# An unused buffer of 320 bytes ahead of the activation tiles: their addresses move by 192 within 512

## What is computed

```python
def swiglu_ffn(x, w_in, w_out):
    gate, up = jnp.split(x @ w_in, 2, axis=-1)       # w_in 1024 x 5632
    return (jax.nn.silu(gate) * up) @ w_out          # w_out 2816 x 1024

def first_block(x, ...):
    for i in range(2):
        if i == 1:
            kv = shared_kv(h, ...)
        h = h + 0.5 * swiglu_ffn(rmsnorm(h, ffn1_norm[i]), ffn1_w_in[i], ffn1_w_out[i])
        hn = rmsnorm(h, mix_norm[i])
        h = h + (short_conv_mixer(hn, ...) if i == 0 else nsa_mixer(hn, ..., kv))
        h = h + 0.5 * swiglu_ffn(rmsnorm(h, ffn2_norm[i]), ffn2_w_in[i], ffn2_w_out[i])
    return h

def second_block(x, ...):
    for layer in range(2):
        h = rms_norm(x, pre_norm[layer])
        m = even_mixer(h, ...) if layer == 0 else odd_mixer(h, ...)
        x = x + rms_norm(m, post_norm[layer])
    return x
```

## The kernel before

| buffers | offset before | after |
|---|---|---|
| raw_a, raw_b, wah, wal, wbh, wbl, hres, cst | 128 | 128 |
| arena, t384 | 160 | 160 |
| rt, rstd, tmp, gate_hid | 320 | 320 |
| hidh, hidl, hnh, hnl, zero, rms | 320 | 128 |
| pbuf, ptb, nmx | 352 | 160 |

## Time and profile before

### The profile page before, as it was taken

One profiled execution on the slowest core, in us unless ns is written; L12 is line 12 of the kernel. 1 busy time (PEld: TensorE's weight loads), 2 busy tenths in 40 slices (PEclk: granted clock), 3 DMA queues, 4 the chain that ended last, 5 costly groups with the idle time before them and its releaser, 6 DMA issues.

```text
span 1378.7 us, 27592 instructions
## 1 busy us (share of the span) xinstructions
PE 1307.9 (95%) x10717; PEld 1248.1 (91%) x10717; DVE 843.6 (61%) x1365; ACT 610.4 (44%) x871; POOL 503.9 (37%) x533
## 2 busy tenths in 40 slices
PE   7999999989999998999999889999999997889878
PEld 6999999989999998999999668999999996788758
DVE  5675458786445566444446784744446586775575
ACT  5343344344334344333335575533334436434381
POOL 3455533315554433444440252444441002600052
PEclk8999999999999999999998899999999999989999
DMA  8787655658676555666644115666653554334300
GB/s 255 210 240 214 202 167 159 185 160 238 204 226 200 168 161 172 204 186 185 183 128 152 36 36 153 184 183 183 183 183 108 153 154 160 111 95 149 124 31 32
DMA packets 275115, 222.52 MB, mean 161 GB/s; under 512 B 8098, under 2 KB 256438, under 8 KB 274924
## 3 DMA queue, kind: packets, MB, share of 16 engines
q1 hardware_dynamic: 272528, 215.59, 51.5%
q0 software_dynamic: 1504, 4.49, 1.6%
q10 hardware_dynamic: 1020, 1.58, 0.4%
HBM read 216.40 MB, written 4.19 MB: 160 GB/s over the span
## 4 chain that ended last, share of the span: by engine, by line
PE 80%; DVE 9%; ACT 5%; POOL 2%; issue 2%; DMA 1%; ACTq 0%; DVEq 0%; SPq 0%; POOLq 0%
PE psum L712 24%; PE psum L713 24%; PE psum L714 24%; DVE wal L1664 2%; DVE hnl L1682 1%; POOL wal L2293 1%; ACT hnh L1294 1%; ACT wah L1213 1%; DVE wal L1847 1%; POOL wbl L2293 1%; ACT pbuf L1461 1%; DVE rstd L1646 1%; PE psum L960 1%; PE psum L914 1%; DVE arena L1725 1%
## 5 line engine op out<-in xcount | busy, mean ns | idle before, releaser
L712 PE MATMUL psum<-hnh,wah 128*128 128x256 f32 (+1 forms) x2176 | 620.3, 285 | 12.2 <-DVE wal L1664 6.6
L713 PE MATMUL psum<-hnl,wah 128*128 128x256 f32 (+1 forms) x2176 | 612.2, 281 | 0.0
L714 PE MATMUL psum<-hnh,wal 128*128 128x256 f32 (+1 forms) x2176 | 611.7, 281 | 0.0
L2293 POOL TENSOR_TENSOR wbl<-raw_b,wbh 128x256 fp32r<-128x256 f32 x412 | 401.6, 1004 | 480.6 <-ACT wbh L1220 409.8
L712 PEld LDWEIGHTS psum<-hnh,wah 128*128 128x128 f32 (+1 forms) x2176 | 416.0, 191 | 18.7 <-issue 12.1
L713 PEld LDWEIGHTS psum<-hnl,wah 128*128 128x128 f32 (+1 forms) x2176 | 414.3, 190 | 2.3 <-issue 1.7
L714 PEld LDWEIGHTS psum<-hnh,wal 128*128 128x128 f32 (+1 forms) x2176 | 415.8, 191 | 0.0
L1664 DVE TENSOR_TENSOR wal<-raw_a,wah 128x2048 fp32r<-128x2048 f32 (+1 forms) x128 | 290.9, 2272 | 101.2 <-ACT wah L1213 99.9
L1213 ACT ACTIVATE wah<-raw_a 128x2048 fp32r<-128x2048 f32 (+1 forms) x126 | 237.2, 1884 | 96.5 <-PE psum L714 81.6
L1332 ACT ACTIVATE gate_hid<-tmp 128x256 f32<-128x256 f32 x88 | 36.7, 417 | 434.7 <-DVE tmp L1782 434.7
L712 PE MATMUL psum<-hidh,wbh 128*128 128x256 f32 x768 | 214.4, 279 | 1.2 <-DVE hidl L1718 1.2
(11 more groups left out here) (304 smaller groups left out, 1468.8 us busy)
## 6 DMA issues: line engine op xcount, KB each, us to landing
raw_a<-in_ffn_w_in SPq DMA_DIRECT2D x176, 512.0 KB, 5.0
raw_b<-in_ffn_w_out SPq DMA_DIRECT2D x88, 512.0 KB, 4.4
raw_a<-in_w_in_even SPq DMA_DIRECT2D x15, 1024.0 KB, 5.3
raw_a<-in_conv_w_in SPq DMA_DIRECT2D x24, 512.0 KB, 3.9
raw_a<-in_w_in_odd SPq DMA_DIRECT2D x11, 1024.0 KB, 5.3
raw_a<-in_w_kv SPq DMA_DIRECT2D x6, 1024.0 KB, 5.5
raw_b<-in_conv_w_out SPq DMA_DIRECT2D x8, 512.0 KB, 5.6
raw_a<-in_attn_w_q SPq DMA_DIRECT2D x4, 1024.0 KB, 5.3
```

Source lines behind the costliest of these rows:

```text
L712: mm(dst, wh, xh, start=start, stop=False)
L713: mm(dst, wh, xl, start=False, stop=False)
L714: return mm(dst, wl, xh, start=False, stop=stop)
L2293: x = g.tensor_tensor(low[:, c], full[:, c], high[:, c].bitcast(F32), ALU.subtract)
```

## The change

One line declares a buffer `spacer` of 80 floats (320 bytes) in each partition between `gate_hid` and `hidh`. No instruction reads or writes it. Every buffer declared after it starts 320 bytes higher, which puts `hidh`, `hidl`, `hnh` and `hnl` on offset 128 within 512 bytes, where the weight tiles are. The instructions of all engines, their order and their waits stay the same; only the addresses in their operands differ. The last buffer still ends inside the memory.

```diff
@@ -145,6 +145,7 @@
         tmp = sb("tmp", [P, 2, 512])
         gate_hid = sb("gate_hid", [P, 4, T])
         silu, hf = gate_hid[:, 0:2], gate_hid[:, 2:4]
+        sb("spacer", [P, 80])
         hidh, hidl = sb("hidh", [P, 2, T], F32R), sb("hidl", [P, 2, T], F32R)
         hnh, hnl = sb("hnh", [P, KT, T], F32R), sb("hnl", [P, KT, T], F32R)
         zero = sb("zero", [P, 512], BF16)
```

## The result

The changed kernel takes 1411.4 us (median of 6 runs, 1410.4 to 1413.4) against 1377.6 us of the kernel before (median of 6, 1371.5 to 1380.6). The ratio is 1.025, with a 95% interval of 1.023 to 1.028: slower, by 34 us, and outside the range that I gave. The runs of the changed kernel also lie closer together, 3 us apart instead of 9.

A forecast was written before the change was run, and what follows sets the result against it. TensorE was taken as the bound, by the number of matmuls and how far apart they start. The terms summed to 0 us against the profiled 1380.5 us, so the median, 1375 us, was forecast, range 1358 to 1398.

The forecast's parts named there:

- the worth of a nanosecond: Lines 712 to 714: about 9504 matmuls, so one nanosecond more or less on each is worth 9.5 us, or 0.7%.
- I take zero, because the strongest row is the first one.: Four feed-forward loops: 113.3 and 117.7 ns at unchanged addresses, so the distance was given 0 us.
- the term for TensorE's operands: Weights and activations of the matmuls going from 192 bytes apart to none: 0 us, bounds -25.0 and +23.2 us.
- The plain f32 rows: Lines 1141 and 1016: steady times across several distances, read as speaking for zero, though not the disputed case.
- The weights of 68 columns: Line 712 with narrower weights: 115.2 ns gaps, read as 64 bytes from the activations and between the two levels.
- rival 1: Float32r matmul stretches: all at the 113 ns pace, giving 1355 to 1362 us, taken as 1360; chance 0.27.
- Readers of the memory don't seem to hold one another up.: Loop windows: other engines use the same memory alike at both paces, a further reason for 0 us.
- Rival 2: Float32r matmul stretches: all at the 118 ns pace, reads colliding from one offset, giving 1397 to 1404 us; chance 0.21.
- from the two paces themselves: Float32r matmuls at distance zero: bounds of -25.0 us and +23.2 us, from every stretch at 113 or 118 ns.
- over 119, would say that the distance matters: Sign in the loops: a pace under 112 or over 119 ns would mean distance matters and both rivals are mis-sized.
- The spread of the runs as one long stretch: Runs at 1373 and 1380 us: differ by one long loop stretch at 118 rather than 113 ns, 6.7 us.
- The moved tiles of other engines: VectorE, ScalarE and GpSimd tiles: some 20 ns an instruction, mostly beside TensorE's work; 0 us, 1 us either way.

The follow-up runs named there:

- late spacer: Against the kernel before, 320 unused bytes placed behind rms, ahead of pbuf, so only the attention buffers move: 1376.7 us against 1375.8, ratio 1.001.
- the kernel at 128: The change's spacer made 448 bytes, so activations start 128 bytes from the weights: 1403.4 us, ratio 1.021 to the kernel before.

## Why the prediction was wrong, point by point

- **What bounds the kernel, and the worth of a nanosecond.** Right in the main. The change is in the pace of lines 713 to 715. The paces and times of all profiled executions lie within 5 us of one line: 114.7 ns as the mean of all gaps under 150 ns between triples in the run with the late spacer (span 1368.7) and 119.9 in the changed kernel (1410.9), 42 us for 5.2 ns, or 8.1 us a nanosecond. I had 9.5. Counted over 9300 gaps the 5.2 ns are 48 us; some 6 came back elsewhere, so "nearly nothing covers TensorE" was a little too strong. The chain has 2 percentage points less of VectorE and 1 less of GpSimd than the earlier trace rows, so a slower TensorE seems to meet work already done that it waited for earlier. That is argued from the two pages, not tested.
- **"I take zero, because the strongest row is the first one."** This is the step that failed. The row was right: two paces at unchanged addresses. The conclusion from it was not, and it put the term for TensorE's operands at 0 us where the runs show 34. That something other than the distance picks between two paces doesn't mean that the distance has no say in which paces there are to pick from. At 192 bytes there are 113.3 and 117.7 ns; at zero there is 120.0 alone. What inside the chip ties the distance to the pace stays open.
- **The plain f32 rows** The earlier trace rows were read correctly and I named their weakness. They don't respond to the distances that they have, and the float32r triples do. The line with 256 columns couldn't have shown much: modulo 256 its distances are only 0 and 128, where the triples are at 120.0 and 118.6 ns. As evidence on the triples the two lines were worth nothing, and I let them count.
- **The weights of 68 columns**, at 115.2 ns: I called this the disputed case at 64 bytes, and read it wrongly. The stationary slice starts 256 bytes into its tile, on 384, and the moving tile on 320; with its sign the distance is -64, which modulo 256 is the old 192. The row held no test of another distance. Why it is neither 113.3 nor 117.7 isn't shown; the narrower load is the likely reason. By the traces the same 24 matmuls have a mean gap of 115.5 ns in the kernel before, 116.8 in the changed one and 120.0 in the kernel at 128, so they do respond to the distance, with values of their own. The first of rival 1's two reasons falls with the reading.
- **"Readers of the memory don't seem to hold one another up."** For the other engines the link is small if there is one: between a mean gap of 114.7 ns (late spacer) and of 119.9 (the change) VectorE's busy time stays at 845 and 844 us, ScalarE's goes from 611 to 615 and GpSimd's from 501 to 497. I also wrote that they are as busy at the one pace as at the other; in the earlier trace rows VectorE has 93 and 83 us at the 113 pace and 78 and 79 at the 118. None of this was a ground for TensorE's own two operands. The Trainium skill's statements (SBUF — State Buffer, "Who interferes with whom", and TensorE: Matmul & The Clock Gate, Part 2) that TensorE never waits for another reader and that its two read ports are independent would have given no change at any distance. The runs go from 113.3 to 120.0 ns, so for float32r triples the measurement decides against the conclusion that operand addresses are free, whatever the ports do.
- **Rival 2** had the direction, with a chance of 0.21. Its idea, that two reads from one offset collide, no run shows or excludes. Its price was mis-sized: I took the 118 pace as the worst there is, since the trace showed no other, and so had 1397 to 1404 us instead of 1411. The bounds "from the two paces themselves" were not bounds. A new level outside the two was named as possible ("over 119, would say that the distance matters") and then given no room in the range.
- **The spread of the runs as one long stretch.** The loops at 117.7 ns change from kernel to kernel at the same distances (the third and fourth before, the second with the late spacer), which fits. But one such stretch was too narrow a reading: in later sets of runs the kernel before went from 1363.2 to 1392.0 us, as if several stretches had been drawn another way (that is argued, for only profiled executions show their paces). The changed kernel, with a single pace, has runs within 3 us.
- **The moved tiles of other engines**: 0 to 1 us. For the attention buffers the late spacer bears it out (ratio 1.001); `hidl` takes 452 ns before and after the change.

## What to carry to other kernels

For back-to-back float32r matmuls of 256 columns with a weight load each, the placement of the moving and the stationary tiles is worth measuring: 32-byte steps of an unused buffer over a period of 256 bytes moved this kernel by up to 2.9%, and the best place can't be guessed from its neighbours. When a trace shows two levels at the same addresses, ask what fixes the levels, not only what picks between them, and don't use them as the bounds of what a new address can cost. An alignment that looks tidy is no argument: here both tiles on one offset was among the worst.

## What the runs showed of the hardware

- The pace of float32r triples (128 stationary columns, 256 moving ones, full granted clock) depends on the address of the moving operand less that of the stationary one, modulo 256 bytes. It was 113.3 to 120.0 ns, with one to three paces in the loops of a placement. Plain f32 matmuls showed no dependence, with 256 columns at distances of 0 and 128 only (one starts every 216 ns).
- At some distances more than one pace is possible (in the loops, two at 32, 192 and 448, three at 160). The stretch takes one when it starts and keeps it for over 1500 matmuls. What picks it is open; so is why 192 is good and 176 and 208 are not.
- With the low weights alone at distance zero, the whole triple lost the pace of 113.3 ns; but blocks of 24 and 48 matmuls on different tiles each kept their own.
